# Cross-attention in a two-layer residual trunk: the query norm moved into the exponential, the key norm moved beside the value projection, on one Trainium2 core

## The reference, cut to what matters

```python
def rms_norm(x, gain):
    y = xf * lax.rsqrt(jnp.mean(xf * xf, axis=-1, keepdims=True) + EPS)
    return (y * gain.astype(jnp.float32)).astype(x.dtype)

def memory_cross_attention(h, mem, mem_norm, w_mq, w_mkv, mq_norm, mk_norm, w_mo):
    mem_h = rms_norm(mem, mem_norm)
    q = rms_norm((h @ w_mq).reshape(B, T, MEM_HEADS, MEM_HEAD_DIM), mq_norm).astype(f32)
    k, v = jnp.split(mem_h @ w_mkv, 2, axis=-1)
    k = rms_norm(k.reshape(B, M, MEM_HEADS, MEM_HEAD_DIM), mk_norm).astype(f32)
    s = jnp.einsum('bthd,bmhd->bhtm', q, k) * (MEM_HEAD_DIM ** -0.5)
    p = jax.nn.softmax(s, axis=-1)
    o = jnp.einsum('bhtm,bmhd->bthd', p, v).reshape(B, T, D).astype(h.dtype)
    return o @ w_mo
```

## Time and profile before

| | us |
|---|---|
| median of 3 executions | 4314.63 |
| lowest and highest | 4312.55 and 4318.15 |
| span of the profiled execution | 4314.6 |
| PE busy in it | 3924.2 |
| DVE busy | 2690.0 |
| POOL busy | 2252.0 |
| ACT busy | 1581.4 |

### The profile page before, as it was taken

The page is one execution under the profiler, slowest core; times in us unless marked ns, Lnnn a source line. Parts: engine busy times, 40 slices in busy tenths (PEclk is TensorE's granted clock), DMA queues, the critical chain, the costliest instruction groups (busy, mean ns, idle before and its releaser), DMA issues.

```text
span 4314.6 us, 56803 instructions
## 1 busy us (share of the span) xinstructions
PE 3924.2 (91%) x18260; PEld 3206.5 (74%) x18260; DVE 2690.0 (62%) x4481; ACT 1581.4 (37%) x2375; POOL 2252.0 (52%) x1722
## 2 busy tenths in 40 slices
PE   7978788999999959999889787889999999599997
PEld 6776666878888848888766766678788888488886
DVE  4456414098998418888754553140989984198886
ACT  3414334334444413333334243343344444133333
POOL 3340342317777667777443403423177776677773
PEclk9988888999999979999999878899999999899999
DMA  3710121144444539999628001211444445399996
GB/s 127 253 69 21 69 98 49 53 152 137 154 141 136 155 102 357 357 351 358 236 99 283 39 20 69 98 49 64 145 137 156 141 135 152 113 377 354 359 348 227
DMA packets 312359, 727.24 MB, mean 169 GB/s; under 512 B 54960, under 2 KB 149264, under 8 KB 306576
## 3 DMA queue, kind: packets, MB, share of 16 engines
q1 hardware_dynamic: 191888, 511.99, 34.9%
q0 software_dynamic: 70464, 139.02, 8.8%
q10 hardware_dynamic: 49856, 74.42, 4.8%
HBM read 605.30 MB, written 119.98 MB: 168 GB/s over the span
## 4 chain that ended last, share of the span: by engine, by line
PE 61%; POOL 11%; issue 10%; DVE 8%; DVEq 3%; ACT 2%; POOLq 2%; DMA 2%; ACTq 1%
PE PS L489 17%; PE PS L490 17%; PE PS L491 17%; POOL gates_dram L1925 7%; POOL w_lo L1856 3%; DMA gates_dram<-gate_value,gate_place 1%; DVEq L1703 1%; PE PS L667 1%; PE PS L653 1%; POOLq L374 1%; ACT junk L959 1%; PE PS L860 1%; PE PS L905 1%; PE PS L543 1%; PE PS L671 1%
## 5 line engine op out<-in xcount | busy, mean ns | idle before, releaser
L1925 POOL DMA_INDIRECT gates_dram<-gate_value,gate_place x768 | 919.2, 1197 | 616.3 <-DVEq L1786 245.2
L489 PE MATMUL PS<-h_hi,u_hi 128*128 128x512 f32 x2048 | 800.0, 391 | 18.7 <-DVE u_lo L1695 11.9
L490 PE MATMUL PS<-h_lo,u_hi 128*128 128x512 f32 x2048 | 798.3, 390 | 0.0
L491 PE MATMUL PS<-h_hi,u_lo 128*128 128x512 f32 x2048 | 798.0, 390 | 0.0
L1856 POOL TENSOR_TENSOR w_lo<-wring,w_hi 128x512 fp32r<-128x512 f32 (+1 forms) x352 | 463.3, 1322 | 602.7 <-ACT w_hi L978 598.8
L489 PE MATMUL PS<-v_hi,g_hi 128*128 128x512 f32 x1536 | 601.1, 391 | 94.4 <-DVE g_lo L1813 94.4
L490 PE MATMUL PS<-v_lo,g_hi 128*128 128x512 f32 x1536 | 600.2, 391 | 0.0
L491 PE MATMUL PS<-v_hi,g_lo 128*128 128x512 f32 x1536 | 599.8, 391 | 0.0
L1271 ACT ACTIVATE u_hi<-u_raw 128x1024 fp32r<-128x1024 f32 x256 | 271.6, 1062 | 756.0 <-PE PS L491 744.9
L1695 DVE TENSOR_TENSOR u_lo<-u_raw,u_hi 128x1024 fp32r<-128x1024 f32 x256 | 312.3, 1221 | 362.5 <-ACT u_hi L1271 350.6
L1316 ACT ACTIVATE v_hi<-v_raw 128x1024 fp32r<-128x1024 f32 x256 | 271.3, 1060 | 624.5 <-PE PS L491 523.7
(11 more groups left out here) (324 smaller groups left out, 6331.3 us busy)
## 6 DMA issues: line engine op xcount, KB each, us to landing
u_raw<-in_expert_u SPq DMA_DIRECT2D x256, 512.0 KB
v_raw<-in_expert_v SPq DMA_DIRECT2D x256, 512.0 KB, 7.4
wring<-in_weights SPq DMA_DIRECT2D x42, 2048.0 KB, 7.9
acts_dram<-act_ring ACTq DMA_DIRECT2D x256, 256.0 KB, 2.2
gates_dram<-zeros SPq DMA_DIRECT2D x6, 8192.0 KB, 54.4
gates<-gates_dram SPq DMA_DIRECT2D x64, 768.0 KB, 7.9
saved<-acts_dram SPq DMA_DIRECT2D x64, 768.0 KB, 12.7
gates_dram<-gate_value,gate_place POOLq DMA_INDIRECT x768
```

Source lines behind the costliest of these rows:

```text
L489: mm(bank_ap, a_hi, b_hi, start=first, stop=False)
L490: mm(bank_ap, a_hi, b_lo, start=False, stop=False)
L491: return mm(bank_ap, a_lo, b_hi, start=False, stop=final)
L1925: g.indirect_dma_start(gates_by_place, bass.IndirectOffsetOnAxis(gate_place[:, t, k:k + 1], 0), gate_value[:, t, k:k + 1], None).then_inc( ...
```

## The change

The stage `S_XNORM` is taken out, on every engine. What it did is divided:

- Queries are no longer multiplied. DVE squares them into `xtmp` while the projection runs. PE sums the squares with the squares as the stationary operand and one column of ones as the moving one (`query_sums`), which gives the 16 sums of a token as 16 columns. ACT turns them into factors (`q_scale`), DVE multiplies these by 1/16, and ACT's exponential takes them as its per-partition scale. DVE scales the maximum by the same column.
- The gain of the queries is multiplied into that of the keys (`kq_gain`).
- Keys are squared by DVE into `k_squares`, summed by PE (`key_sums`), turned into factors by ACT (`key_and_query_factors`), spread by PE (`key_factors`) and multiplied by DVE, all within `S_XPROJ`, beside the value groups. `query_sums` comes after chunk 1 and `key_sums` after chunk 5 of the first value group, `key_factors` after chunk 4 of the second. On ACT the factors come before the copies of the first value group.
- Six semaphores are added, all on the list `local`.

```diff
+        q_scale = stats[:, 240:256]
+        kq_gain = stats[:, 28:30]
+        k_squares = area("k_squares", 0, DC, MEM)
+        k_rows = area("k_rows", 18432, MEM)
...
 
-        (S_NORM1, S_PROJ, S_KQ, S_INV, S_SCAN, S_ONORM, S_FOX, S_OUT1, S_NORM2, S_XPROJ, S_XNORM,
-         S_XATT, S_OUT2, S_NORM3, S_PQ, S_PICK, S_PEER) = range(17)
+        (S_NORM1, S_PROJ, S_KQ, S_INV, S_SCAN, S_ONORM, S_FOX, S_OUT1, S_NORM2, S_XPROJ,
+         S_XATT, S_OUT2, S_NORM3, S_PQ, S_PICK, S_PEER) = range(16)
...
                 for s in range(2):
                     weight_group(DC * (2 * PAIR_MK + s), 4, channel_tile(s * 4, (mem_hi, mem_lo), MEM), xg_done,
                                  free=lambda m: (xg_stored, s * 4 + m + 1), x_chunk=lambda c: XP_MEM + c // 2 + 1)
+                def query_sums():
+                    pe.wait_ge(xg_stored, 16)
+                    pe.wait_ge(q_squared, DC)
+                    for t in range(NT):
+                        for h in range(MH):
+                            i = t * MH + h
+                            for e in range(2):
+                                last = mm(PS[:, 7, i:i + 1], xtmp[:, 2 * h + e, t * P:(t + 1) * P], ones[:, 0:1], start=e == 0, stop=e == 1)
+                    last.then_inc(q_summed, 1)
+
+                def key_sums():
+                    pe.wait_ge(k_squared, MH)
+                    for i in range(DC):
+                        last = mm(PS[0:NROW, 6, 0:MEM], to_row(i // 2), k_squares[:, i, :], start=i == 0, stop=i == DC - 1)
+                    last.then_inc(k_summed, 1)
+
+                def key_factors():
+                    pe.wait_ge(k_rows_ready, 1)
+                    for h in range(MH):
+                        mm(PS[:, 4 + h // 2, (h % 2) * MEM:(h % 2 + 1) * MEM], sel(h, NROW), k_rows[0:NROW, :],
+                           start=True, stop=True).then_inc(k_spread, 1)
+
+                def beside_values(s, c):
+                    if (s, c) == (0, 1):
+                        query_sums()
+                    if (s, c) == (0, 5):
+                        key_sums()
+                    if (s, c) == (1, 4):
+                        key_factors()
+
                 for s in range(2):
                     weight_group(DC * (2 * PAIR_MV + s), MT, token_tile(s * 2, (mem_hi, mem_lo), 512), xg_done,
-                                 free=lambda m: (xg_stored, 8 + s * 2 + m + 1))
+                                 free=lambda m: (xg_stored, 8 + s * 2 + m + 1), after_chunk=lambda c: beside_values(s, c))
                 stage_end(pe, l, S_XPROJ)
-                for i in range(2 * MH):
-                    n = SEQ if i < MH else MEM
-                    k = 20 + i
-                    pe.wait_ge(sq_ready, k + 1)
-                    for e in range(2):
-                        last = mm(PS[0:NROW, i // MH, 0:n], to_row(i % MH), xtmp[:, 2 * (k % 2) + e, 0:n],
-                                  start=i % MH == 0 and e == 0, stop=i % MH == MH - 1 and e == 1)
-                    last.then_inc(ss_done, 1)
-                spread_rows(20, 3, [[sel(i, NROW)] for i in range(MH)], xtmp[0:NROW, 4, :])
-                for i in range(MH):
-                    pe.wait_ge(normed, 20 + i + 1)
-                    mm(PS[:, 2 + i % 4, 0:MEM], sel(i, NROW), xtmp[0:NROW, 5, 0:MEM], start=True, stop=True).then_inc(bc_done, 1)
-                stage_end(pe, l, S_XNORM)
 
                 FI = NT * FH
 
...
                 split_first(l, PAIR_MQ, x_hi, hT)
                 for i in range(DC // 2):
                     fn(mem_hi[:, 2 * i:2 * i + 2, :], memT[:, 2 * i:2 * i + 2, :], ACT.Copy).then_inc(x_hi_ready, 1)
+                def key_and_query_factors():
+                    act.wait_ge(q_summed, 1)
+                    act.wait_ge(k_summed, 1)
+                    fn(q_scale, PS[:, 7, 0:NT * MH], ACT.Ln, bias=eps_col, scale=1.0 / (2 * P))
+                    fn(k_rows[0:NROW, :], PS[0:NROW, 6, 0:MEM], ACT.Ln, bias=eps_col[0:NROW], scale=1.0 / (2 * P))
+                    act.drain()
+                    fn(k_rows[0:NROW, :], k_rows[0:NROW, :], ACT.Exp, bias=zero_col[0:NROW], scale=-0.5)
+                    fn(q_scale, q_scale, ACT.Exp, bias=zero_col, scale=-0.5)
+                    act.drain().then_inc(k_rows_ready, 1)
+
                 group_banks = [range(4), range(4, 8), range(8, 12), range(12, 16), range(16, 18), range(18, 20)]
                 for g, banks in enumerate(group_banks):
                     split_w(l, PAIR_MQ + g // 2, g % 2, LATE)
                     if g + 1 < len(group_banks):
                         split_w(l, PAIR_MQ + (g + 1) // 2, (g + 1) % 2, EARLY)
+                    if g == 4:
+                        key_and_query_factors()
                     for b in banks:
                         act.wait_ge(xg_done, b + 1)
                         if b < 8:
...
                         else:
                             fn(vx[:, b % 2, (b - 16) // 2 * 512:((b - 16) // 2 + 1) * 512], PS[:, b - 16, :], ACT.Copy).then_inc(xg_stored, 1)
                 stage_end(act, l, S_XPROJ)
-                act.wait_ge(ss_done, 20 + 2 * MH)
-                for i, n in enumerate((SEQ, MEM)):
-                    inv_norms(xtmp[0:NROW, 4 + i, 0:n], PS[0:NROW, i, 0:n], 1.0 / (2 * P), zero_col[0:NROW])
-                act.drain().then_inc(rs_ready, 1)
-                stage_end(act, l, S_XNORM)
                 FI = NT * FH
 
                 def mem_transposed(i):
                         fn(xtmp[:, 6 * (i % 3 == 2) + i % 3 % 2, 0:MEM], PS[:, SCORE_BANKS[i % 3], 0:MEM], ACT.Exp, bias=nmax[:, i:i + 1],
-                           scale=(2 * P) ** -0.5, accum_out=rsum[:, i:i + 1]).then_inc(exp_ready, 1)
+                           scale=q_scale[:, i:i + 1], accum_out=rsum[:, i:i + 1]).then_inc(exp_ready, 1)
                     if 1 <= i <= n_items:
                         mem_transposed(i - 1)
...
                 stage_end(dve, l, S_NORM2)
                 split_x(XP_MQ, x_lo, hT, x_hi)
                 split_x(XP_MEM, mem_lo, memT, mem_hi, 2)
+                v.tensor_tensor(kq_gain, par[:, PC["mq"]:PC["mq"] + 2], par[:, PC["mk"]:PC["mk"] + 2], ALU.mult)
+                for b in range(DC):
+                    dve.wait_ge(xg_stored, b + 1)
+                    v.tensor_tensor(xtmp[:, b, :], qx[:, b, :], qx[:, b, :], ALU.mult).then_inc(q_squared, 1)
+                for h in range(MH):
+                    dve.wait_ge(xg_stored, DC + 2 * h + 2)
+                    pair = kx[:, 2 * h:2 * h + 2, :]
+                    v.tensor_tensor(k_squares[:, 2 * h:2 * h + 2, :], pair, pair, ALU.mult).then_inc(k_squared, 1)
+                dve.wait_ge(k_rows_ready, 1)
+                v.tensor_scalar(q_scale, q_scale, (2 * P) ** -0.5, None, ALU.mult)
+                for h in range(MH):
+                    dve.wait_ge(k_spread, 2 * (h // 2) + 2)
+                    for e in range(2):
+                        k_e = kx[:, 2 * h + e, :]
+                        v.scalar_tensor_tensor(k_e, k_e, kq_gain[:, e:e + 1], PS[:, 4 + h // 2, (h % 2) * MEM:(h % 2 + 1) * MEM], ALU.mult, ALU.mult)
                 stage_end(dve, l, S_XPROJ)
-
-                def x_square(i):
-                    k = 20 + i
-                    src = (qx if i < MH else kx)[:, 2 * (i % MH):2 * (i % MH) + 2, :]
-                    n = SEQ if i < MH else MEM
-                    if i >= 2:
-                        dve.wait_ge(ss_done, k - 1)
-                    v.tensor_tensor(xtmp[:, 2 * (k % 2):2 * (k % 2) + 2, 0:n], src, src, ALU.mult).then_inc(sq_ready, 1)
-
-                for i in range(2 * MH):
-                    x_square(i)
-                for i in range(2 * MH):
-                    n = SEQ if i < MH else MEM
-                    dve.wait_ge(bc_done, 20 + i + 1)
-                    for e in range(2):
-                        t_e = (qx if i < MH else kx)[:, 2 * (i % MH) + e, :]
-                        last = v.scalar_tensor_tensor(t_e, t_e, pcol("mq" if i < MH else "mk", e), PS[:, 2 + i % 4, 0:n], ALU.mult, ALU.mult)
-                    dve.drain().then_inc(normed, 1)
-                stage_end(dve, l, S_XNORM)
                 FI = NT * FH
 
                 def mem_normalise(i):
-                    v.tensor_scalar(nmax[:, i:i + 1], nmax[:, i:i + 1], (2 * P) ** -0.5, None, ALU.mult).then_inc(max_ready, 1)
+                    v.tensor_scalar(nmax[:, i:i + 1], nmax[:, i:i + 1], q_scale[:, i:i + 1], None, ALU.mult).then_inc(max_ready, 1)
                     if i:
...
-                for k, pairs in ((S_OUT1, [PAIR_OUT]), (S_NORM2, []), (S_XPROJ, [PAIR_MQ, PAIR_MK, PAIR_MV]), (S_XNORM, []), (S_XATT, []),
+                for k, pairs in ((S_OUT1, [PAIR_OUT]), (S_NORM2, []), (S_XPROJ, [PAIR_MQ, PAIR_MK, PAIR_MV]), (S_XATT, []),
```

More of the change, by code:

```diff
@@ L344, in trunk_kernel @@
         gemm_done = lsem("gemm_done")
+        q_squared, k_squared, q_summed, k_summed = lsem("q_squared"), lsem("k_squared"), lsem("q_summed"), lsem("k_summed")
+        k_rows_ready, k_spread = lsem("k_rows_ready"), lsem("k_spread")
```

## The result

| | before | after |
|---|---|---|
| median, executions beside each other on one chip (us) | 4316.39 | 4286.47 |
| lowest and highest | 4312.55 and 4320.54 | 4282.38 and 4290.88 |
| span of the profiled execution | 4314.6 | 4281.0 |

After divided by before is 0.9931, with a 95% interval of 0.9917 to 0.9945. The change makes the kernel about 30 us faster. 4285 was predicted.

The account below looks back on a forecast made before the run. PE bounds the value groups; the norm stage lies wholly on the path. 4314.6 - 66.8 + 29.8 (PE work) + 0.8 (clears) - 4.0 (attention start) = 4274.4, plus 11.0 for the clock's fall: 4285.4 us, range 4282 to 4289; 8 in 10, 4270 to 4296.

Parts of the forecast that it names:

- the mechanism taken as likeliest: PE's clock falls to half within the query sums, costing 5.5 us a layer (3.7 to 7.4); chance 0.53.
- 64 passes of query sums at full clock: On PE in the first value group: 64 passes 0.115 us apart, 7.4 us a layer.
- key sums: On PE: eight matmuls, 16 passes of 256 moving columns, 3.5 us a layer.
- pause before chunk 4: Second value group: PE stalls 2.3 us because ACT's factors delay its copy of chunk 4's weights.
- key factors: On PE in the second value group: four matmuls, eight passes of 256 columns, 1.7 us a layer.
- stretch at full clock: Time from the first matmul of the first value group to the first score, 38.8 us a layer.
- fall: within the sums: Query-sum passes left after the clock falls take twice as long: 3.6 us more a layer at the middle.
- fall: chunks behind them: Value chunks after the query sums run at half clock until it rises: 1.9 us a layer (1.5 to 2.4).
- clock at the attention's start: First score passes run at full clock once the old pause is gone: 2.0 us less a layer (0 to 2.7).
- What is removed: The norm stage between value copies and scores: 32.6 us in the first layer, 34.2 in the second, together 66.8.
- The rival in which loads don't overlap: Each query-sum pass takes 0.258 us, 9.1 us a layer more, giving 4293 us; chance 0.07.
- second fall: Stall, a chunk and 24-row key factors let the clock fall again: about 2.5 us a layer more, 4290; chance 0.12.

Follow-up runs that it names:

- 128 columns: Against the kernel after, each query-sum pass moved 128 columns in place of one, in one block; 4275.24 us, ratio 0.9898 to the kernel before.
- its repetition: The kernel after run once more without edit, beside the kernel before on the same chip; 4291.65 us, ratio 0.9935.
- the spread kernel: Against the kernel after, the 64 query-sum passes were spread behind chunks 1 to 7 of the first value group; 4272.75 us, ratio 0.9890.
- the added pause: Against the kernel after, eight unused squares on DVE followed the key multiplications, so PE waited before the scores; 4313.31 us, ratio 0.998.
- the kernel with a block of 32 passes and the cut factors: Against the kernel after, DVE added channel blocks, leaving 32 query-sum passes in one block, and ACT's Ln and Exp were separated between chunk copies; 4274.26 us, 0.9881.

## Why the prediction came out

The median is 4286.5 against 4285, and the mechanism taken as likeliest is what the traces show. Term by term, for a layer, with what each addition costs between the first matmul of one chunk and that of a later one, beyond the 1.40 us of a plain chunk:

| term | predicted | measured |
|---|---|---|
| 64 passes of query sums at full clock | 7.4 | 7.1 (128 columns) |
| key sums | 3.5 | 3.8 |
| pause before chunk 4 | 2.3 | 1.9 (1.7 of it idle) |
| key factors | 1.7 | 2.2 |
| these four together | 14.9 | 15.0 |
| stretch at full clock | 38.8 | 38.8 (128 columns) |
| fall: within the sums | 3.6 | 1.9 and 4.3 |
| fall: chunks behind them | 1.9 | 1.3 and 2.1 |
| clock at the attention's start | -2.0 | -1.9 and -1.8 |

- **What is removed.** Right. The stretch before, less the stage (56.48 - 32.6 = 23.9), plus the 14.9 of new work, is 38.8 us. The kernel with 128 columns, in which the clock holds, has 38.83. That the four terms of the new work come out at 15.0 with 14.9 said is in part luck: two were 0.3 and 0.4 too high, two 0.3 and 0.5 too low. The two that were low left out the change to the 24-row matmuls and back: their first pass starts 0.33 us behind the last large matmul's start, where large ones are 0.23 apart, and the chunk behind them takes 1.51 us, not 1.40.
- **Query sums at full clock.** Mis-sized by 0.3 us a layer. The price came from L793's passes with 64 columns. Passes with one column are 0.003 us closer. The rival in which loads don't overlap is out: 0.112 is below half of 0.258. By the rule that the Trainium skill gives in "TensorE: Matmul & The Clock Gate", Part 3: Packing small matmuls, loads of all 128 rows would not have overlapped; the trace does not agree. (The same section also has loads pulled ahead when they go to a background weight buffer; with that the trace would agree.)
- **The clock.** The step that decided was to let two stretches at 0.50 speak against the busy share. It held in every block of 64 passes with 1 or 32 columns. By the Trainium skill, same page, Part 1: The HAM clock gate, taken as the profile's busy time, the clock would have stayed up; PE was busy 6.00 of 6.00 us at 0.50, so it does not agree when taken so. The size came out at 3.2 to 6.4 us a layer where 5.5 (3.7 to 7.4) was said, so one layer lies below the stated ends. The working put the fall 2.4 to 5.2 us after the start of the sums, from the two pauses of the norm stage. (The slice with 0.90 puts the first of them at 624.8, not 624.9, which makes it 2.3 to 5.3.) In the kernel after and its repetition it came some 2.4 to 5.0 us after it. A block of 64 passes is caught early or late, and the two profiled executions differ by 3.2 us through that. How much of the 8.5 us between the lowest and the highest time after it explains is not shown: the executions of the spread kernel, whose profiled one has no fall there, differ by 11.2 us.
- **The pause before chunk 4.** Mis-sized by 0.4 us, of the right kind. ACT's factors fit: its value copies began 4.55 us after the group's start (4.6 predicted). The copy of chunk 4's weights began 0.2 us earlier than said, since ACT's instructions overlap. The 1.37 us a chunk for POOL was not its own pace. One of its instructions takes 1.27 to 1.29 us in both kernels; in those rows each waited for ACT's copy, and so for PE's 1.40 us a chunk. With four copies ready they follow each other after 4.97 / 4 = 1.24 us. PE's four chunks lasted 5.7 us by their starts, not 5.6.
- **Key factors and their cover.** Right in kind: DVE's last multiplication ends at 625.21, before PE's last value matmul at 627.2. DVE took 3.22 us, not 3.85. One multiplication lasts 0.47 us in both kernels. In the kernel before a drain stood behind the two of each head, and the pairs started 1.0 us apart; in the kernel after, without it, they start 0.8 apart.
- **No second fall.** The rival with one (0.12) did not come: from 601 to 627 the clock is 1.00, with the pause and the eight 24-row passes inside.
- **The attention's start.** Right, and shown by the added pause: 1.5 and 1.7 us come back with it. The scale as a column was put at nothing. The first Exp takes 0.56 us at 629.98, where the kernel before has 0.47, and it lies on the way to the first transposes: 0.1 of the 0.14 us by which 3.39 exceeds the 3.25 that was said.
- **Semaphore clears.** 0.8 us in all were counted. In the traces the clears of a layer take 7.55 and 7.54 us before and 7.92 us after, from the first to the last: 0.75 us more in all, as counted. No run leaves them out.

Set against the profiled execution, the sum of 4285.4 is 4.4 us above the span of 4281.0. The stretches come out 1.3 shorter than said (87.3 in place of 2 x (38.8 + 5.5) = 88.6): the first layer's fall was put 2.3 too dear and the second layer's 0.9 too cheap. Untouched parts are 2.5 shorter, the clears were counted at 0.8, and the transposes give 0.3 back. The median lies closer to the forecast than the profiled execution does. That it is within 1.5 us of it is chance, with a fall that comes at varying times. Even the range of 4282 to 4289 is narrower than what the kernel's own executions do: two of four are near 4290.5, and the repetition on another chip has a median of 4291.65. What the runs bear out is the sum and its mechanism, to a few us.

## What to carry to other kernels

Work that is moved off a serial stage onto the bound engine costs its full length there, so count it in passes, and check what it does to that engine's clock: here 64 passes with one moving column, in one block, cost 3.2 to 6.4 us a layer beyond their 7.1. Put such passes in pieces between large matmuls, but end them before the next engine needs the sums. Do the halving (an addition on DVE) where an engine has nothing to do; it took 3.6 us of query sums from PE in a layer, and 1.7 us of key sums.

## What the runs showed of the hardware that I had not expected

- A block of passes that shows PE and its loads 100% busy can still run into half clock. With 1 and with 32 moving columns it did in each of eight blocks of 64 passes, with 128 in neither of two.
- The block that fell was not always long. With 32 passes, 3.6 us at full clock, the clock fell within the block in the second layer of two kernels. In the first layer of one it fell 1.2 us behind the block, while the large matmuls ran, and in that of the other it held. In pieces of 2 to 12 passes between large matmuls it held in all eight layers that were profiled.
- When the fall comes is not fixed for a kernel. In the same program it came some 5 us or under 3 us after the first pass (so the "6 us or more" of one expectation was not needed), and the two layers of one execution can differ.
- An f32 matmul with a full weight load takes 2 x 0.112 us when such matmuls follow one another, with one moving column and with 128 alike (start to start in the blocks, at a clock of 1.00).
- The price of the fall goes with the time at 0.50: 6.8 us of it cost 3.2, and 13.7 us cost 6.4. In the first layer of the kernel with a block of 32 passes and the cut factors, 3.4 us cost 1.5.
